# The opening of a two-block transformer kernel joined with its first projection: modulation by row pairs, two weight parts outside the ring, four tiles multiplied pair by pair

## What is computed

```python
mod = silu(c) @ mod_w[layer] + mod_b[layer]        # 6 x 1024 values for each of the two streams
h   = rmsnorm(x, norm1_g[layer]) * (1 + scale) + shift
p   = h @ w_in[layer]                              # q, k, v, recurrence, convolution
```

## Time and profile before

| | us |
|---|---|
| median of 3 runs | 2868.94 |
| lowest and highest run | 2860.03 and 2869.28 |
| span of the profiled execution | 2861.5 |

### The profile page before, as it was taken

One profiled execution on the slowest core, in us unless ns is written; L12 is line 12 of the kernel. 1 busy time (PEld: TensorE's weight loads), 2 busy tenths in 40 slices (PEclk: granted clock), 3 DMA queues, 4 the chain that ended last, 5 costly groups with the idle time before them and its releaser, 6 DMA issues.

```text
span 2861.5 us, 50422 instructions
## 1 busy us (share of the span) xinstructions
PE 2699.6 (94%) x21334; PEld 2275.9 (80%) x21334; DVE 1932.5 (68%) x2291; ACT 1475.9 (52%) x1748; POOL 104.8 (4%) x74
## 2 busy tenths in 40 slices
PE   6998898999999978789999999999999899989999
PEld 4875776888778768678888888888888779988999
DVE  3365866322444767578898989888898667666766
ACT  3345243212333533367777777777777445454544
POOL 1100000000013000010000000000000000000000
PEclk9999999999999989899999999999999999999999
DMA  8514101322225240089999999999998334542453
GB/s 321 230 59 181 66 3 59 110 96 97 95 90 203 76 156 4 3 339 361 339 368 340 360 345 353 359 339 368 357 359 345 151 118 175 181 159 94 165 189 118
DMA packets 81803, 581.79 MB, mean 203 GB/s; under 512 B 9272, under 2 KB 11072, under 8 KB 11840
## 3 DMA queue, kind: packets, MB, share of 16 engines
q1 hardware_dynamic: 78336, 571.48, 53.1%
q10 hardware_dynamic: 3264, 7.33, 0.7%
HBM read 577.73 MB, written 1.05 MB: 202 GB/s over the span
## 4 chain that ended last, share of the span: by engine, by line
PE 83%; DVE 8%; ACT 4%; issue 2%; DMA 1%; PEldq 1%; POOL 0%; DVEq 0%; POOLq 0%; ACTq 0%; PEld 0%; SPq 0%
PE banks L2522 21%; PE banks L2548 11%; PE banks L2900 9%; PE banks L1077 9%; PE banks L857 8%; PE banks L1103 4%; PE banks L891 4%; PE banks L1534 3%; PE banks L3250 2%; PE banks L2097 1%; DVE ring_split L307 1%; PE banks L522 1%; PE banks L2532 1%; DMA ring<-parts 1%; PE banks L2936 1%
## 5 line engine op out<-in xcount | busy, mean ns | idle before, releaser
L2729 DVE TENSOR_TENSOR ring_split<-ring,arena_split 128x2048 fp32r<-128x2048 f32 x336 | 770.0, 2293 | 113.6 <-ACT arena_split L2641 105.9
L2641 ACT ACTIVATE arena_split<-ring 128x2048 fp32r<-128x2048 f32 x336 | 644.4, 1919 | 57.7 <-PE banks L2548 57.6
L307 DVE TENSOR_TENSOR ring_split<-ring,arena_split 128x2048 fp32r<-128x2048 f32 x140 | 321.3, 2295 | 322.9 <-ACT arena_split L301 322.9
L301 ACT ACTIVATE arena_split<-ring 128x2048 fp32r<-128x2048 f32 x142 | 270.8, 1908 | 98.0 <-PE banks L1077 74.0
L2522 PE MATMUL banks<-arena_split 128*128 128x512 f32 x896 | 301.3, 399 | 6.6 <-DVE ring_split L2729 6.6
L2548 PE MATMUL banks<-arena_split 128*128 128x512 f32 x896 | 297.3, 392 | 7.3 <-DVE arena_split L2760 7.2
L2522 PE MATMUL banks<-arena_split,mix_split 128*128 128x512 f32 x896 | 303.7, 401 | 0.0
L2548 PEld LDWEIGHTS banks<-arena_split 128*128 128x128 f32 x896 | 168.2, 188 | 50.0 <-issue 10.8
L2522 PEld LDWEIGHTS banks<-arena_split 128*128 128x128 f32 x896 | 169.7, 189 | 42.2 <-DVE ring_split L2729 7.0
L857 PE MATMUL banks<-mix_split,ring_split 128*128 128x256 f32 x704 | 199.0, 283 | 0.0
L857 PE MATMUL banks<-h_split,arena_split 128*128 128x256 f32 x704 | 197.6, 281 | 0.0
(11 more groups left out here) (419 smaller groups left out, 5403.3 us busy)
## 6 DMA issues: line engine op xcount, KB each, us to landing
ring<-parts SPq DMA_DIRECT2D x541, 1024.0 KB, 4.8
arena<-bias ACTq DMA_DIRECT2D x2, 2048.0 KB, 8.9
x_buf<-xt SPq DMA_DIRECT2D x1, 2048.0 KB, 7.9
constants<-con SPq DMA_DIRECT2D x1, 1952.0 KB, 14.6
out<-x_buf ACTq DMA_DIRECT2D x4, 256.0 KB, 2.2
arena<-lora ACTq DMA_DIRECT2D x2, 256.0 KB, 5.1
arena<-gate ACTq DMA_DIRECT2D x2, 256.0 KB, 5.3
arena<-sgw ACTq DMA_DIRECT2D x2, 256.0 KB
```

What stands on the lines that cost most here:

```text
L301: act.activation(high[:, m % depth, :], slots[:, n % RING, :], ACT.Copy).then_inc(w_high.h, w_high.one(times))
L307: dve.tensor_tensor(low_slots[:, n % RING, :], slots[:, n % RING, :], high[:, m % high.shape[1], :].bitcast(F32), ALU.subtract).then_inc(w ...
L2641: act.activation(high[:, m % 3, :], slots[:, m % RING, :], ACT.Copy).then_inc(wh_ok.h, 1)
L2729: dve.tensor_tensor(low_slots[:, m % RING, :], slots[:, m % RING, :], high[:, m % 3, :].bitcast(F32), ALU.subtract).then_inc(wl_ok.h, 1)
```

## The change

The phase `modulation` and its `end_phase` are gone, and so is the one behind the first transfers. A class `Opening` does their work inside `first_mixers(0)`, with the products of tiles 0 to 3:

- The modulation parts are stored in HBM as pairs (shift, scale) of the same 256 channels, so that one pair gives shift and scale of two rows of tokens.
- Weight parts 0 and 1 are loaded into the arena (`raw`), not into the ring, behind modulation pairs 0 and 1. They are split by quarters of 128 x 512 (two rows), ACT high, DVE low.
- The sum of squares is made with the squares as stationary operand and one column of `mean_d`: 32 products 128 x 1, the root and its inverse on 128 x 4, and four products that spread it over bank 4.
- The waits at the start are apart: first constants, each half of the tokens, `par1`, `fold`.
- DVE multiplies a row with the inverse root only (L704), ACT applies gain and shift in place (L671) and makes the high half (L675), DVE the low one (L732).
- PE multiplies pair by pair: `row_pair`, `turn`, and `products(m, part)`, 12 multiplications for two rows and the two tiles of a part.
- Weight parts 0 and 1 no longer count in `used`; `apart` is 2, and `split_part_high(act, 2)` stands ahead of the evictions of tiles 0 to 3. It waits on `freed`, which is `place[2] + 1 - 1`. With `first_part` 8, `place` is 6, 7, 10, 13, 16, ...
- The transfer of the attention bias is issued behind tile 3, and the large constants behind six parts instead of two.

The core of the diff:

```diff
+    class Opening:
+        def on_sp(self, sp):
+            load_parts(sp, 2)
+            sp.dma_start(self.raw[:, 0, :], parts[0, :, :]).then_inc(self.landed[0].h, 16)
+            load_parts(sp, 2)
+            sp.dma_start(self.raw[:, 1, :], parts[1, :, :]).then_inc(self.landed[1].h, 16)
+            load_parts(sp, 4)
+        def on_pe(self, pe, terms):
+            def products(m, part):
+                pe.wait_ge(self.part_low[part].h, self.part_low[part].at(m + 1))
+                for k in (2 * m, 2 * m + 1):
+                    pe.wait_ge(t_low.h, t_low.at(k + 1))
+                    for t in (2 * part, 2 * part + 1):
+                        terms(t, k)
+            pe.wait_ge(self.con_ready.h, 16)
             for k in range(KT):
+                pe.wait_ge(self.squared.h, self.squared.at(k + 1))
+                for b in range(self.BLOCKS):
+                    mm = pe.matmul(bank(b)[:, 0:1], self.sq[:, k, b * P:(b + 1) * P], C("mean_d")[:, 0:1],
+                                   start=k == 0, stop=k == KT - 1)
...
+            self.row_pair(pe, 0)
+            self.turn(pe, 0)
+            products(0, 0)
+            self.row_pair(pe, 1)
+            products(0, 1)
+            self.turn(pe, 1)
+            self.row_pair(pe, 2)
+            products(1, 0)
+            self.turn(pe, 2)
+            self.row_pair(pe, 3)
+            products(1, 1)
+            self.turn(pe, 3)
+            for m in (2, 3):
+                for part in range(2):
+                    products(m, part)
...
+        def on_act(self, act):
...
+            copy(0)
+            quarter(0, 0)
+            tokens(0)
+            quarter(0, 1, 2, 3)
+            quarter(1, 0)
+            copy(1)
+            quarter(1, 1)
+            tokens(1)
+            copy(2)
+            quarter(1, 2, 3)
+            tokens(2)
+            copy(3)
+            tokens(3)
+            act.wait_ge(self.late.h, 16 * DEPTH)
+        def on_dve(self, dve):
...
+            scale(0, 1)
+            dve.wait_ge(self.par_ready.h, 16 * DEPTH)
+            quarter(0, 0)
+            store(0)
+            scale(2, 3)
+            low(0)
+            scale(4, 5, 6, 7)
+            quarter(0, 1, 2, 3)
...
+            quarter(1, 0)
+            store(1)
+            quarter(1, 1)
+            low(1)
+            quarter(1, 2)
+            store(2)
+            quarter(1, 3)
+            low(2)
+            store(3)
+            low(3)
...
         def split_part_high(act, m):
-            split_high(act, high, place[m], m, freed=place[m - depth] + 1 if m >= depth else None)
+            split_high(act, high, place[m], m, freed=place[max(m - depth, apart)] + 1 - (m < apart + depth) if m >= depth else None)
...
+            if opened:
+                opened.on_act(act)
+                split_part_high(act, apart)
+            else:
+                tokens.on_act(act, copy_rows)
+                for m in range(max(ahead, 1), depth):
+                    split_part_high(act, m)
+                load_bias()
...
             for t in range(QKV):
                 tile_out(t)
+                if opened and t == 3:
+                    load_bias()
```

More of the change, by code:

```diff
@@ L2819, in first_mixers @@
         owner = ["act"] * 16 + ["dve"] * 10 + ["act"] * 2 + ["dve"] * 2
-        closes = [t + 1 == n_tiles or part_of[t + 1] != part_of[t] for t in range(n_tiles)]
+        ends = [t + 1 == n_tiles or part_of[t + 1] != part_of[t] for t in range(n_tiles)]
+        apart = 2 if opened else 0
+        closes = [ends[t] and part_of[t] >= apart for t in range(n_tiles)]
         bank_no = [(0, 1, 2, 3, 5, 6)[t % 6] for t in range(QKV)] + [5 + t % 2 for t in range(QKV, n_tiles)]
@@ L2826, in first_mixers @@
         since = 0 if front else 1
-        place = [first_part + 2 * front + p + 2 * min(max(p - since, 0), early - front) for p in range(n_parts)]
-        stream["got"] += n_parts + 2 * early
+        place = [first_part + 2 * front + p - apart + 2 * min(max(p - since, 0), early - front) for p in range(n_parts)]
+        stream["got"] += n_parts - apart + 2 * early
         mod = Modulation([(0, 16, 48), (1, 0, 16)] if l == 0 else [(1, 16, 48)],
@@ L2831, in first_mixers @@
                          [place[m + since] + 1 + j for m in range(early - front) for j in range(2)])
+        if opened:
+            stream["ahead"] = apart
         high, depth, ahead = mixer_high, HIGHS, stream["ahead"]
@@ L2886, in terms @@
                 if p not in weights:
-                    weights[p] = [v3(x, KT) for x in take_split_part(pe, high, place[p], p)]
+                    weights[p] = opened.weights(p) if p < apart else [v3(x, KT) for x in take_split_part(pe, high, place[p], p)]
                 wh, wl = weights[p]
@@ L2954, in _ @@
                 mod.half(pe)
-            for kk in range(KT):
-                if tokens:
-                    pe.wait_ge(t_low.h, t_low.at(kk + 1))
[L2958 to L2962, removed]
+            if opened:
+                opened.on_pe(pe, terms)
+                modulate(3)
+            else:
+                for kk in range(KT):
+                    pe.wait_ge(t_low.h, t_low.at(kk + 1))
+                    for t in range(2):
+                        terms(t, kk)
+                    if front and kk % 2:
+                        mod.half(pe)
+            for t in range(2 * max(apart, 1), QKV):
                 tile(t)
@@ L2987, in copy_rows, with load_bias @@
                     mod.copy(act, m)
[L2988 to L2991, removed]
+            def load_bias():
+                act.dma_start(bias, bias_in[l, :, :].rearrange("p (q k) -> p q k", k=LAT)).then_inc(b_in.h, 16)
+            if opened:
+                opened.on_act(act)
+                split_part_high(act, apart)
+            else:
+                tokens.on_act(act, copy_rows)
+                for m in range(max(ahead, 1), depth):
+                    split_part_high(act, m)
+                load_bias()
             def tile_out(t):
@@ L3078, in _ @@
         def _(dve):
[L3079 to L3083, removed]
+            if opened:
+                opened.on_dve(dve)
+                split_low(dve, high, place[apart], apart)
+            else:
+                tokens.on_dve(dve)
+                for m in range(max(ahead, 1), depth):
+                    split_low(dve, high, place[m], m)
             own_pad, side = S("conv_pad"), S("shift_side")
@@ L3089, in next_low @@
             def next_low(t):
-                m = part_of[t] + depth
-                if closes[t] and m < n_parts:
+                m = next_part(t)
+                if m is not None:
                     split_low(dve, high, place[m], m)
@@ L3747, in build @@
     lat = (CTX, T)
-    stat = Squares((0, T), 0, folded=False)
     entry = lambda l, stat: Normed(stat, (0, T), gain1(l), lambda t, s: modc(l, t, s))
-    tokens = entry(0, stat)
-    modulation([(0, 0, 16)], ready, x_loaded, late, tokens, mixer_high)
+    opened = Opening(con_ready, par_ready, fold_ready, tokens_loaded, late)
     for l in range(DEPTH):
@@ L3832 @@
     mod = [list(cols_of(w)) for w in i["mod_w"]]
-    parts += mod[0][:8]
+    opening = list(cols_of(i["w_in"][0][:, :2 * UNIT]))
+    parts += opening + [mod[0][w * 4 + m] for m in range(4) for w in range(2)]
     for l in range(DEPTH):
@@ L3841 @@
             m = FRONT[l] + p - (not FRONT[l])
-            parts += [part] + (rows[2 * m:2 * m + 2] if FRONT[l] <= m < EARLY[l] else [])
+            parts += ([part] if l or p >= len(opening) else []) + (rows[2 * m:2 * m + 2] if FRONT[l] <= m < EARLY[l] else [])
         parts += rows[2 * EARLY[l]:]
```

199 lines of the change are left out of this document (139 added, 60 removed).

## The result

| | before | after |
|---|---|---|
| median of 20 runs, us | 2865.74 | 2875.55 |
| lowest and highest | 2860.03 and 2872.58 | 2866.19 and 2882.99 |
| span of the profiled execution | 2861.5 | 2875.4 |

The ratio is 1.0029, with a 95% interval of 1.0021 to 1.0037: by it the change makes the kernel 8.3 us slower (6.0 to 10.6); the two medians are 9.8 us apart. The forecast was 2.1 us faster, 2866.8; the time lies at the upper end of its range of 2858 to 2876, where the first rival put it (+5, 2874, up to 2879). The median before, 2868.94 for three runs, came out at 2865.74 for twenty.

A forecast was written before the change was run, and what follows sets the result against it. TensorE, busy 94% of the span, was taken as the bound. Tile 3 earlier, the wait ahead of tile 4 and the half clock gave -8.4 + 4.3 + 2.0 = -2.1 us, from 2868.9 to 2866.8; range 2858 to 2876.

The forecast's parts named there:

- the first rival: Slower: one-column sums don't raise the clock; sum 15.4 us, tile 3 near 67; +5, 2874, up to 2879; chance 0.22.
- the clock in the sum of squares: Start of the kernel: 3.5 us at half clock, then full clock; sum takes 9.4 us, from 8.4 until 17.9.
- pair 0: First modulation pair, behind the sum and its spread: starts at 19.6 against 24.61 before, ends at 21.5.
- The rival's condition that loads don't depend on the clock: Faster rival, at the sum: loads independent of the clock, or clock not lost when idle; -4 to -8, about 2863; chance 0.14.
- From pair to tokens: Opening, from the end of pair 0 to its first products: 5.3 us, so these start at 26.8.
- The first 12 products: Products of pair 0's tokens, behind 4 us of TensorE idle: at half clock, 5.0 us, to 31.8.
- the 12 products behind the second idle stretch: Products of pair 1's tokens, ready at 41.1 after 1.9 us of idle: full clock, 2.7 us.
- The stall: Ahead of tile 4: TensorE waits 4.3 us, to 66.7, for the split of weight part 2, held by `used`.
- The half clock behind it: Tiles 4 and 5 start at half clock behind the wait: costs 2.0 us, bounds 0 and 2.8.
- Hidden work: Opening and later: transfers for pair 3 hidden by 11 us, bias and masks (ending by 100) by 25 us.
- The rest: Everything behind tile 5: same instructions, bound by TensorE, so the shift of the opening stays.
- The other two rivals: Faster: loads independent of clock or clock not lost, about 2863, chance 0.14; wait on `used` costs nothing, 2860.5, chance 0.04.

The follow-up runs named there:

- The wide sum: Changed kernel with its sums of squares made as before, 8 products of 512 columns and no spread: 2869.31, ratio 1.0006 to the kernel before.
- the kernel with both edits: Changed kernel with the split's wait on the count lowered to 8 and the sums 512 columns wide: 2862.58, ratio 0.9982 to the kernel before.
- the warmed run: Changed kernel with ten unused products of 128 columns ahead of the one-column sums: 2875.02, ratio 1.0029 to the kernel before.
- the run with the count at 8: Changed kernel with the split of weight parts 2 and 3 waiting only for the eight parts of the opening: 2872.47, ratio 1.0015 to the kernel before.
- the late bias: Kernel before with only the bias transfer issued behind tile 3 and the large constants behind six parts: 2869.18, ratio 1.0001 to the kernel before.
- the last filled kernel: Changed kernel with count 8, sums 512 columns wide, six and two unused products in TensorE's idle stretches, VectorE's shift-weight instructions moved later: 2858.59, ratio 0.9972.
- the shifted kernel: Kernel before with six unused products of 512 columns ahead of tile 4: 2875.63, ratio 1.0027 to the kernel before.
- its two variants: Kernel before with the bias and large constants transferred later (2869.18), and kernel before with six unused products ahead of tile 4 (2875.63).

## Why the prediction was wrong

**The step that failed is the clock in the sum of squares.** I took 3.5 us at half clock and then the full one, as the rows of the 512-column sum showed, for products of one column, and wrote "its queue is full all the time" as the reason. The queue was full, and the clock stayed at 1.2 GHz: 13.80 us where 9.4 stood. TensorE began at 7.77 and not 8.4, so the end came 3.7 us late. The spread took 2.05 instead of 1.1 and pair 0, still partly at half clock, 2.90 instead of 1.9, so pair 0 ended at 27.16 against 21.5. The wide sum, begun at the same time, shows it by contrast: it ends at 17.17, before the 17.9 of the forecast, and pair 0 behind it runs at full clock, as the stretch of the kernel with both edits shows (32 of its 33 passes are pair 0's, and all 33 took 2.01 us):

```profile
17.00:19.30 2.30, 2.01 (x33) 0.94 (x32) 1.39 (x1) 0.91 (x2) 0.00 (x0) 1.00 1.02 425
```

**Rule against rows.** The rival's condition that loads don't depend on the clock is refuted: in the warmed run the same load took 0.192 us at 2.4 GHz and 0.333 at 1.2. The Trainium skill, page "TensorE: Matmul & The Clock Gate", section on LDWEIGHTS, gives a load as its columns over 1.2, in ns, with no term for the clock; for 128 columns that is 0.107 us, an estimate of mine from that page. The traces disagree with it at both levels.

**From pair to tokens** was 5.62 instead of 5.3 (ScalarE's token rows 2.07 for 1.71). The first 12 products took 4.71 (5.0 expected). A miss of its own: I gave the 12 products behind the second idle stretch the full clock, 2.7, and they took 4.59, with PEclk 0.69 from 47 to 52 us. TensorE had waited only 2.2 us there. So tile 3 ended at 67.94 instead of 60.5, 7.4 late: 3.7 (sum) + 1.0 (spread) + 1.0 (pair 0) + 0.3 (tokens) - 0.3 (first 12 products) + 1.9 (the 12 behind the second idle stretch) are 7.6.

**The stall** was right in place, cause and size: 4.3 expected, 4.4 measured (69.86 to 74.24), and the run with the count at 8 removes it. The half clock behind it cost 12.76 - 11.24 = 1.5, against 2.0. So -2.1 + 7.4 + 0.1 - 0.5 is +4.9, and 5.0 was measured at the milestone.

**Hidden work** was right: no wait for pair 3, weights or bias shows among TensorE's waits, and the late bias shows no cost. The masks ended at 102.8 (82.22 + 20.60) and not by 100, far ahead of their first reader. One reading behind it was wrong: the 6.95 us of the earlier trace rows are a transfer in the chain and not a wait of TensorE, which was busy with pairs 1 and 2 during most of it and idled 0.45 us for weights:

```profile
33.98 1.93 PE L522 MATMUL banks<-ring,condition_buf 128*32 128x256 f32 x32 [0.45 <-DMA ring<-parts]
```

The sum doesn't use the 6.95. Two smaller slips don't move it either. The product of 0.228 us comes to 0.233 by its own working (18.9 / 81). And a span is 1.8 us shorter than the time of the same execution (2875.4 and 2877.24 for the changed kernel), so the profiled execution before lay some 5.6 us below the median of three and not 7.4.

**The rest** ("the same instructions, so the shift stays") held to 240 us, and by the medians to within the 3 us left open. In the first pair of profiles it did not hold.

**The rivals.** The first one was what happened: its price (+6.0 and +1.5 at tile 3, which would end near 67, then +5 in all) stood there, and the place to decide it (0.34 or 0.19 between 12 and 18 us) too. I gave it 0.22, because I took a busy queue as evidence for the clock, with no row of a one-column product to bear that out. That its numbers came so close is partly luck. Its sum of 15.4 us was 1.6 too long, and it had neither the slower spread (1.0) nor the half clock behind the second idle stretch (1.9); these partly cancel. And 2875.6 lies near its 2874 also because the kernel before turned out 3.2 us faster than its first three runs; its +5 is what the milestone shows, and 8.3 what the ratio does.

The other two rivals did not occur: loads followed the clock, the clock was lost in this kernel's idle stretches, and the split of part 2 waited for the count, as the chain shows at 69.95.

## What to carry to other kernels

Where TensorE is idle or cold, cost a product by what it did to the clock in a row of the same shape; for a shape that no row shows, the case that it doesn't raise the clock is an equal one. Turning a reduction round, so that the data become the operand that is loaded, saves columns but makes it a run of loads: 13.8 us and 2.05 for the spread, against 9.3 us and 3.36 for the inverse on VectorE. Check what a renumbered count releases: two parts that no longer count moved a split of 4.2 us from beside the products to in front of them. And before a difference of a few us is followed through two profiles, take a second profile of the same kernel.

## What was not expected of the hardware

- Products of one column with a 128 x 128 load each left TensorE at 1.2 GHz through 13.80 us without a gap, and in the warmed run the clock fell at 11.0 us, in the middle of them, with PE and PEld busy 4.00 of 4.00 us on both sides of the fall.
- Behind an idle stretch of 2.2 us the clock was down in the next 12 products (4.59 us), while the 12 behind pair 1 ran at full clock (2.98). Behind one of 1.8 us in the last filled kernel it was up. The gaps of 0.5 us ahead of a turn cost it in no run.
- At full clock an f32 product of 512 columns took 0.9 us, two passes (12 passes in 5.35 us in the shifted kernel); one of the reduced format 0.234.
- The same kernel, profiled twice, had rests of 2788.4 and 2784.3 us, with 126 and 109 us of them at 1.2 GHz. At the start, the same sum of squares took 8.81, 9.16, 10.00 and 8.50 us in the four profiles of the kernel before and its two variants. The Trainium skill, page "TensorE: Matmul & The Clock Gate", Part 1, says that the number of slow products at a start varies from run to run; the sums here agree, and the rests show such a scatter in the middle of a kernel.
